# Prompt attention in head pairs inside the decode sequences, with page turns in three rotating half banks and the first pages loaded during the q projection

## The reference

```python
q = rms_norm((xn @ w_q).reshape(B, T, H, Dh), q_norm)
s = einsum('bqhd,bkhd->bhqk', q, k) * scale + f_q[..., None] - f_key
s = where(k_pos <= q_pos, s, -inf)
o = einsum('bhqk,bkhd->bqhd', softmax(s), v)          # then h += o @ w_o
# prompt: k, v are the 256 new tokens; f is the running sum of the log forget values
# decode: k, v = 1024 cached tokens (8 pages of 128, found through page_table) + 8 new ones
```

## Time and profile before

| | |
|---|---|
| median of 3 runs | 1751.15 us (1748.93 to 1753.79) |
| the profiled execution | 1752.86 us, span 1751.2 us |
| TensorE busy, of the span | 94% |
| VectorE, ScalarE, GpSimd busy | 57%, 37%, 5% |
| moved by DMA | 254.95 MB, 146 GB/s on average |
| granted TensorE clock, mean | 0.97 of full |

### The profile page before, as it was taken

The page is one execution under the profiler, slowest core; times in us unless marked ns, Lnnn a source line. Parts: engine busy times, 40 slices in busy tenths (PEclk is TensorE's granted clock), DMA queues, the critical chain, the costliest instruction groups (busy, mean ns, idle before and its releaser), DMA issues.

```text
span 1751.2 us, 37118 instructions
## 1 busy us (share of the span) xinstructions
PE 1648.4 (94%) x15372; PEld 1531.5 (87%) x15372; DVE 992.6 (57%) x1578; ACT 651.4 (37%) x935; POOL 90.3 (5%) x132
## 2 busy tenths in 40 slices
PE   6999999999999999999999999997778888999997
PEld 5999998988998999999889999984555566999997
DVE  5655437857774665544585555466744444655532
ACT  4343325643334543433433343331323332534320
POOL 0000000012212000000014300000000000000000
PEclk9999999999998999999999999996889998999999
DMA  6444462410002644444444444431079995444441
GB/s 188 146 156 155 133 180 73 145 61 16 16 16 59 190 145 144 148 152 146 131 156 152 150 154 146 154 102 48 13 290 350 352 371 185 145 145 156 149 143 62
DMA packets 206844, 254.95 MB, mean 146 GB/s; under 512 B 17914, under 2 KB 188074, under 8 KB 206586
## 3 DMA queue, kind: packets, MB, share of 16 engines
q1 hardware_dynamic: 202714, 246.38, 41.5%
q0 software_dynamic: 4016, 6.88, 1.4%
HBM read 246.89 MB, written 6.35 MB: 145 GB/s over the span
## 4 chain that ended last, share of the span: by engine, by line
PE 81%; DVE 10%; DMA 5%; ACT 2%; issue 2%; SPq 0%; POOL 0%; DVEq 0%; POOLq 0%
PE ps L691 20%; PE ps L692 20%; PE ps L690 20%; PE ps L945 7%; PE ps L940 4%; DMA ring<-in_cache_k 4%; PE ps L1253 2%; DVE ring_r L1658 2%; PE ps L1238 1%; ACT ring_r L1320 1%; DMA arena<-in_x_sample 1%; PE ps L1233 1%; DVE xn_r L1673 0%; PE ps L1126 0%; PE ps L805 0%
## 5 line engine op out<-in xcount | busy, mean ns | idle before, releaser
L690 PE MATMUL ps<-arena_r,ring_r 128*128 128x320 f32 x2032 | 632.5, 311 | 5.1 <-DVE xn_r L1673 3.1
L692 PE MATMUL ps<-arena_r,ring_r 128*128 128x320 f32 x2032 | 629.4, 310 | 0.0
L1658 DVE TENSOR_TENSOR ring_r<-ring,ring_r 128x2048 fp32r<-128x2048 f32 (+1 forms) x130 | 291.4, 2242 | 247.9 <-ACT ring_r L1320 144.9
L690 PEld LDWEIGHTS ps<-arena_r,ring_r 128*128 128x128 f32 x2032 | 383.1, 189 | 8.3 <-DVE ring_r L1658 3.5
L692 PEld LDWEIGHTS ps<-arena_r,ring_r 128*128 128x128 f32 x2032 | 383.1, 189 | 0.0
L691 PE MATMUL ps<-arena_r,ring_r 128*128 128x320 f32 x1136 | 351.0, 309 | 0.0
L691 PE MATMUL ps<-xn_r,ring_r 128*128 128x320 f32 x896 | 278.6, 311 | 0.0
L691 PEld LDWEIGHTS ps<-arena_r,ring_r 128*128 128x128 f32 x1136 | 213.3, 188 | 0.2
L1658 DVE TENSOR_TENSOR arena_r<-arena,arena_r (+3 forms) x155 | 141.9, 923 | 110.8 <-ACT arena_r L1320 49.5
L690 PE MATMUL ps<-arena_r 128*128 128x320 f32 x592 | 183.2, 309 | 0.0
L692 PE MATMUL ps<-arena_r 128*128 128x320 f32 x592 | 182.9, 309 | 0.0
(11 more groups left out here) (316 smaller groups left out, 2000.4 us busy)
## 6 DMA issues: line engine op xcount, KB each, us to landing
ring<-in_ffn_w_in SPq DMA_DIRECT2D x67, 1024.0 KB, 5.0
ring<-in_cache_k SPq DMA_DIRECT2D x64, 512.0 KB, 6.2
arena<-in_cache_v SPq DMA_DIRECT2D x64, 512.0 KB, 7.6
ring<-in_ffn_w_out SPq DMA_DIRECT2D x24, 1024.0 KB, 5.1
arena<-in_ffn_w_in SPq DMA_DIRECT2D x21, 1024.0 KB, 5.0
ring<-in_rw_w_rkv SPq DMA_DIRECT2D x11, 1024.0 KB, 5.1
ring<-in_ffn_w_out SPq DMA_DIRECT2D x12, 768.0 KB, 4.4
arena<-in_ffn_w_out SPq DMA_DIRECT2D x8, 1024.0 KB, 5.1
```

The source lines that it names most:

```text
L690: pe.matmul(out, part(s, 1)[:, k, cs], x_hi, start=first_, stop=False)
L692: return pe.matmul(out, part(s, 0)[:, k, cs], x_hi, start=False, stop=last)
L1658: return TT(out, x, high.bitcast(F32), ALU.subtract)
```

## The change

- `fox` leaves the list of tiles. The prompt attention of heads 2b and 2b+1 is done inside sequence b of the decode, in bank 6 (`FOX`), with semaphores of its own. The loops over sequences are written out on TensorE, ScalarE and VectorE.
- The scores read `q_f` and `kT` of the head's 64 partitions directly, without block-diagonal copies. The forget sums are kept as three fp32r parts in 48 rows for each half of the array (`nF`, `head_pick`) and enter by one fp32r matmul. A new tile `nf_rep` and eight small VectorE steps in `query_forgets` build them. `head_sel` and its DMA are gone.
- The values of a pair are written to the two partition halves of the bank and leave in one copy; `oT` is split block by block (`out_high`, `out_low`).
- Half page n (n = 2 for each page) goes to bank 3 + n % 3, instead of two pairs of banks.
- Seven value pages are loaded when `down2` is done, key pages 0 to 3 after the first slab of q, and pages 0 and 1 are turned before `q_rep`. The first two `fo` slabs are loaded after q and split within sequences 0 and 1.

```diff
@@ tiles and constants
+    add("nf_rep", 1)
-    add("fox", 3 * H)
+    m["fsel"] = (i[:, None] < H) & (i[:, None] == hd[None, :]) & (part[None, :] < 3)
+    m["fpart"] = part[:, None] == np.arange(3)[None, :]
+    m["fpick"] = (part[:, None] < 3) & (hd[:, None] == np.arange(H)[None, :])
+        PAGE_BANKS, FOX, OUT = 3, 6, 7
+        def page_bank(b, j, half):
+            return PAGE_BANKS + (2 * (b * PAGES + j) + half) % 3
@@ SyncE
+            sp.wait_ge(tile_done, first["down2"] + DT)
+            for j in range(PAGES - 1):
+                load_values_first(j)
+            sp.wait_ge(tile_done, first["q"] + 2)
+            for j in range(4):
+                load_k(0, j, page_of(0, j))
+            sp.wait_ge(S("page_space"), 1)
+            load_values_first(PAGES - 1)
+            for q in range(2):
+                s = first_slab["fo"] + q
+                load_slab(s, cols(dense["fo"], 0, DT, 256 * q, 256))
+                free_after(s, tile_done, first["fo"] + 2 * q + 2)
+            for j in range(4, PAGES):
+                load_k(0, j, page_of(0, j))
+            for j in range(4):
+                load_k(1, j, page_of(1, j))
+            with sp.Fori(1, BS - 1) as b:
                 load_sequence(b, False)
@@ TensorE
+            end(mmul(bank(t, TP), K("fsel")[0:H, :], FT_[:, 0:TP]))
+            def turn_page(b, j):
+                G = b * PAGES + j
+                pe.wait_ge(S(f"k_page{j % 4}"), b * 32 + 16 * (j // 4 + 1))
+                for half in range(2):
+                    if half == 0 and G >= 2:
+                        pe.wait_ge(S("kT_dve"), G - 1)
+                    if half == 1 and G >= 1:
+                        pe.wait_ge(S("kT_act"), G)
+                    for m in range(4):
+                        mm = pe.transpose(ps[:, page_bank(b, j, half), m * P:(m + 1) * P],
+                                          k_page(j % 4)[:, (4 * half + m) * P:(4 * half + m + 1) * P], ident)
+                mm.then_inc(S("k_page_free"), 1)
+            turn_page(0, 0)
+            turn_page(0, 1)
+            page_evicted(2, 2)
+            head_rep("q_rep", rs)
+            dve_done(first["q_rep"] + DT - 1)
+            turn_page(0, 2)
+            turn_page(0, 3)
+            def fox_scores(hd):
...
+                pe.matmul(ps[:, FOX, 0:3 * P], head_pick[pr, hd:hd + 1].to_broadcast([HD, P]), nF[pr, :],
+                          start=True, stop=False, skip_group_check=True)
+                pe.matmul(ps[:, FOX, 0:P], q_f[pr, m, 0:P], kT[pr, m, 0:P], start=False, stop=False,
                           skip_group_check=True)
+                pe.matmul(ps[:, FOX, P:3 * P], q_f[pr, m, P:2 * P], kT[pr, m, 0:2 * P], start=False, stop=True,
+                          skip_group_check=True).then_inc(S("fox_scores"), 1)
+            def fox_turn(hd):
+                pe.wait_ge(S("p_ready"), hd + 1)
+                if hd % 2:
+                    pe.wait_ge(S("fox_pT"), hd)
+                else:
+                    pe.wait_ge(S("fox_scored"), hd + 2)
...
+            def fox_values(m):
+                pe.wait_ge(S("fox_pT"), 2 * m + 2)
...
             def unit_scores(b, u):
-                pe.wait_ge(S("kT_act"), b * PAGES + (2 * u + 4))
-                pe.wait_ge(S("kT_dve"), b * PAGES + (2 * u + 4))
+                page_evicted(b * PAGES + 2 * u + 2, b * PAGES + 2 * u + 2)
@@ TensorE, one sequence
                 unit_scores(b, 0)
                 turn_page(b, 4)
                 turn_page(b, 5)
+                fox_scores(2 * b)
                 unit_scores(b, 1).then_inc(S("half_scored"), 1)
                 turn_page(b, 6)
+                fox_scores(2 * b + 1)
                 turn_page(b, 7)
                 unit_scores(b, 2)
                 unit_scores(b, 3)
...
+                fox_turn(2 * b)
                 if not last:
                     turn_page(b + 1, 0)
+                fox_turn(2 * b + 1)
+                if not last:
                     turn_page(b + 1, 1)
...
+                fox_values(b)
                 if not last:
                     turn_page(b + 1, 2)
@@ ScalarE, one sequence
+                page_copy(b, 4)
+                page_copy(b, 5)
+                fox_exp(2 * b)
+                page_copy(b, 6)
+                fox_exp(2 * b + 1)
+                page_copy(b, 7)
                 act.wait_ge(S("less_max"), b + 1)
...
+                out_high(b)
+                if not last:
                     page_copy(b + 1, 3)
+                if b < 2:
+                    hi(first_slab["fo"] + b)
@@ VectorE
-            copy_out("q", q_f, between=(lambda: later_pages(0), lambda: later_pages(1), query_forgets), norm_name="mix1")
+            copy_out("q", q_f, 2, between=(lambda: later_pages(0), lambda: later_pages(1), query_forgets), norm_name="mix1")
@@ VectorE, one sequence
+                page_copy(b, 4)
+                page_copy(b, 5)
+                fox_scored(2 * b)
+                page_copy(b, 6)
+                fox_scored(2 * b + 1)
+                page_copy(b, 7)
                 dve.wait_ge(S("half_scored"), b + 1)
                 dve.tensor_reduce(sst[:, 0:1], ps[:, 0, :], AX.X, ALU.max)
+                probabilities(2 * b)
...
+                probabilities(2 * b + 1)
+                fox_columns(2 * b)
                 if not last:
                     page_copy(b + 1, 0)
+                fox_columns(2 * b + 1)
+                if not last:
                     page_copy(b + 1, 1)
...
+                fox_out(b)
                 if not last:
                     page_copy(b + 1, 2)
                     queries(b + 1)
...
+                out_low(b)
...
+                if b < 2:
+                    lo(first_slab["fo"] + b)
```

More of the change, by code:

```diff
@@ L1187, in _ @@
             end(mmul(bank(t, TS), K("selcol")[0:H, :], FT_[:, TP:T]))
+            t = first["nf_rep"]
+            begin(t)
+            end(mmul(bank(t, TP), K("fsel")[0:H, :], FT_[:, 0:TP]))
             gemm("q", xn_hi, xn_lo, xn_ready("mix1"), "mix1")
             head_totals("q_norm", q_sq, S("q_sq"))
-            head_rep("q_rep", sg[:, 1, :])
-            pe.wait_ge(S("head_sel_in"), 16)
-            pe.wait_ge(S("nF_ready"), 1)
-            def scores(hd):
-                t = first["fox"] + fox_tile(hd, 0)
-                begin(t)
-                pe.wait_ge(S("qp_ready"), hd // 2 + 1)
-                qp = qp_bd[:, hd // 2 % 2, hd % 2, :]
-                pe.matmul(bank(t, 384), head_sel[:, hd, :], nF_dup, start=True, stop=False, skip_group_check=True)
-                pe.matmul(ps[:, t % 8, 0:P], qp[:, 0:P], kT[:, hd // 2, 0:P], start=False, stop=False,
-                          skip_group_check=True)
-                end(pe.matmul(ps[:, t % 8, P:3 * P], qp[:, P:2 * P], kT[:, hd // 2, 0:2 * P], start=False, stop=True,
-                              skip_group_check=True))
@@ L1223, in _, with page_evicted @@
-            for kind, hd in fox_order:
-                (scores, turn, values)[kind](hd)
+            def page_evicted(act_n, dve_n):
+                pe.wait_ge(S("kT_act"), act_n)
+                pe.wait_ge(S("kT_dve"), dve_n)
+            def turn_page(b, j):
[10 more added lines that the diff above has]
+                mm.then_inc(S("k_page_free"), 1)
@@ L1297, in sequence @@
                 pe.wait_ge(S("o_own"), b * 2 + 2)
-                pe.transpose(ps[:, 7, 256:384], o_two, ident).then_inc(S("o_turned"), 1)
-            dve_done(first["fox"] + 3 * H - 1)
-            for j in range(4):
-                turn_page(0, j)
-            with pe.Fori(0, BS - 1) as b:
-                sequence(b, False)
-            sequence(BS - 1, True)
-            pe.wait_ge(S("o_split"), 2)
+                pe.transpose(ps[:, OUT, 256:384], o_two, ident).then_inc(S("o_turned"), 1)
+            pe.wait_ge(S("o_split"), BS + 1)
             gemm("fo", oT_hi, oT_lo)
@@ L1556, in _, with head_roots @@
             ffn(1)
-            def head_roots(name, src_name, src, dst, sq_sem, norm_name):
+            def head_roots(name, src_name, src, dst, sq_sem, norm_name, ahead=4, out=None):
                 for q in range(4):
-                    hi(first_slab[src_name] + q + 2)
+                    if q < ahead:
+                        hi(first_slab[src_name] + q + 2)
                     if q == 0:
@@ L2295, in _, with fox_columns, fox_out @@
-            dve.wait_ge(dve_freed, freed["d"][first["fox"] + 3 * H])
-            dve.wait_ge(S("o_hi"), 1)
-            low(oT_lo[:, :, 0:TP], oT[:, :, 0:TP], oT_hi[:, :, 0:TP]).then_inc(S("o_split"), 1)
+            def fox_columns(hd):
+                dve.wait_ge(S("fox_turned"), hd + 1)
+                CP(pT[:, hd % 2, :], ps[:, FOX, 0:3 * P]).then_inc(S("fox_pT"), 1)
+            def fox_out(m):
+                dve.wait_ge(S("fox_values"), m + 1)
+                CP(oT[:, m, 0:TP], ps[:, FOX, 0:TP]).then_inc(S("fox_out"), 1)
@@ new lines, in out_low, with queries @@
+            def out_low(m):
+                dve.wait_ge(S("o_hi"), m + 1)
```

(26 more changed lines are left out.)

292 lines of the change are left out of this document (122 added, 170 removed).

## The result

The changed kernel took 1697.86 us, the median of 4 runs (1694.73 to 1700.72), against 1752.06 us for the kernel before in the same session. The ratio is 0.9692 with an interval of 0.9668 to 0.9716: 3.1% faster, 54 us. The forecast was 1707, range 1682 to 1727.

A forecast was written before the change was run, and what follows sets the result against it. The decode was taken as set by page transfers, TensorE close behind. `fo` begins at 1195.5 + 197.4 + 30.6 + 1 + 4.5 = 1429.0 instead of 1473.57, 44.6 us earlier: 1707 us, range 1682 to 1727.

The forecast's parts named there:

- the walk: TensorE's work and waits followed in order through one decode sequence with a pair of prompt heads; 28.2 us against 24.00.
- Period: Time of one decode sequence, from `unit_scores(b, 0)` to the next; 28.2 us predicted, seven of them 197.4.
- The stall of page 5: In each sequence, the upper half of page 5 waits for ScalarE's copy of page 4's lower half; 0.45 us.
- Step 6: Late in each sequence: head turn, page turns, transposes of p and `fox_values` (1.50 us), reaching 22.2 us.
- The wait for the turned head: In each sequence, TensorE idles 2.0 us while VectorE does `probabilities(2b+1)` and `fox_columns(2b)` before the head's turn.
- Clock: Allowance of 4.5 us because the first decode sequence would begin at TensorE's lower level, 1.2 GHz.
- Pages still pace it: Rival: in the decode, key pages end the waits and the period is 25.5 us; 1685 us, chance 0.13.
- A drain at each tile shape: Rival: switches to 64-row scores and 64-column values each drain TensorE, decode 8 us longer; 1715 us, chance 0.10.
- Low clock in the first sequences: Rival: TensorE at the lower clock through the first sequences, some 20 us more; 1727 us, chance 0.08.
- Slower: Rival: lower clock all through the decode because new 2 us gaps recur; 1867 us, chance 0.03.
- nothing: Rival: a decode period near 33.8 us eats the 44.6 us gain; chance 0.01.
- steps 3 to 5: Sequence waits: page 4's copy 0.45 us, page 7's copy behind the exponentials 1.0, VectorE before the head's turn 2.0.

The follow-up runs named there:

- copy7_first: The changed kernel with ScalarE copying page 7 ahead of the exponentials of head 2b+1; 1692.12 us, ratio 0.9654.
- values_128: The changed kernel with the pair's values computed on all 128 weight columns, one head after the other, two copies out; 1705.74 us, ratio 0.9728.
- no_prompt: The changed kernel with the prompt attention left out of the sequences, its block of oT filled with zeros; 1680.55 us, ratio 0.9585.
- reordered2: The changed kernel with page copies, head turns, probabilities, pair values and the turn of `o_two` reordered across TensorE, ScalarE and VectorE; 1677.75 us, ratio 0.9572.
- late_pages: The changed kernel with key pages 0 to 3, all eight first value pages and `fo` issued only at `page_space`; 1711.88 us, ratio 0.9764.
- fp32_forget: The changed kernel with the forget part of the prompt scores in fp32 instead of fp32r; 1706.62 us, ratio 0.9752.

## Why the prediction was right

The mechanism was right: the waits of the walk stand where it put them, and pages no longer end them. The result was 9 us high. More than half of that, 5.5 us, are two allowances beside the walk that were not needed (4.5 for the clock, 1 for the splits); the rest are sizes taken a little large. One reading of the earlier trace rows was wrong, that a new tile shape has no price, and the walk hit some numbers by luck; both are told below.

- **First unit.** Predicted 1195.5, measured 1195.37. This close a hit is luck, since two errors cancel: the q product ended at 1181.4 instead of 1179.8, and the turns of pages 0 and 1 and `q_rep` ran faster than priced, at full clock (granted 1.00 up to 1191.90, `q_rep` 1.36 us). Behind the wait of 3.26 us the clock was down as priced: pages 2 and 3 took 3.47 us at a granted clock of 0.52.
- **Period.** 28.2 against 27.56 (the later ones 27.64, and the seventh 29.25). To the end of the new tokens' scores 13.8 was walked and 13.74 is measured, and that too is luck in part: the two stalls are shorter by 0.5 and the scores' own matmuls by 0.2, while the old work around them takes 0.6 more than the 10.17 of the earlier trace rows, where a wait or a new tile shape cuts a group. In it the fp32r pass is 0.28, not 0.18: the row of a 320-column projection matmul did not carry over to this one. The stall of page 5 is 0.25 for 0.45, the one for page 7 is 0.71 for 1.0. `copy7_first` shows the latter's cause.
- **Step 6** is the part of the walk most mis-sized: `fox_values` 0.81 for 1.50. I took twice the price of a head from the earlier trace rows, whose matmuls follow one another on the whole array. `values_128` shows that working in two column halves in turn makes the difference. The wait for the turned head is 1.65 for 2.0, by the same order on VectorE as walked.
- **Clock.** 4.5 us were set aside for the first sequence, and it cost 0: granted clock 1.00 from 1195.37 to 1222.94. The prediction held both views, 4.5 us in the sum and "2.4 GHz from the first sequence on" among its signs; the second came true. The seventh sequence (29.25, granted 0.94) and the last (29.05, granted 0.90) pay instead, some 1.6 us in the seventh.
- **Last sequence.** 30.6 predicted, 29.05 measured, with the idle at the place named (2.52) and the lower clock behind it. The two splits of `fo` cost nothing that shows, where I had 1.
- **Sum.** 197.4 + 30.6 + 1 + 4.5 = 233.5 was set against 224.1 measured: 2.4 from the seven periods, 1.5 from the last, 1 and 4.5 from the rest. These make 9.4 and, with 0.1 at the first unit, 9.5 at `fo`; of that, 0.5 is gone again by the end.

**The rivals.** *Pages still pace it*: no, since no page is waited for; but in `no_prompt` they do at once, and `reordered2` is at the edge. *A drain at each tile shape*: true in kind, though not in size. The three products of a head take 1.02 us from the first start to the next group's (1199.28 to 1200.30, and 1202.97 to 1203.99), less than the 1.1 of the sum. But their neighbours got longer. Eight transposes hold TensorE for 0.93 us ahead of a group of 128x128 (1203.99 to 1204.92) and for 1.03 ahead of the 64-row scores (1201.94 to 1202.97). The first group of a unit takes 0.64 behind the scores (1200.30 to 1200.94) and 0.54 behind a page turn (1204.92 to 1205.46). And the 64-column values start 0.20 behind the last transpose of p, where the 128-column ones of `values_128` start after 0.11. That is about 0.1 us at each of four places, 0.4 a sequence and some 3 us in all, where the prediction gave the rival 8. This agrees with the Trainium skill, page "TensorEngine Tiling (Array Packing)", section "Key Properties", which the prediction named, as far as that a change of tiling mode has a cost. *Low clock in the first sequences*: not in this kernel; in `late_pages` it stands behind a wait of 8.99 us (granted 0.72 from 1213 to 1230). *Slower* and *nothing*: the three new waits of steps 3 to 5 came out below their price, and `fp32_forget` shows that work added there comes through once, 0.94 a sequence, and does not multiply.

**Where the gain came from.** The attention of the prompt, some 70 us on the path, costs 17 where it lies beside the pages (`no_prompt`). Around it three smaller pieces each carry a part, measured by undoing that one: early pages 14 us by the medians, `fo` out of q 14 (some 10 in the trace), the forget sums in one pass 8.8 (7.5 by the periods). They cannot be added up, for each was undone alone.

**Open.** How much of the 54 us the cheaper attention (no block-diagonal queries, one fp32r pass, 64-column values) would give in its old place, ahead of the decode: no run has it there. And what makes the clock fall in one sequence and not in the next. In the kernel before it held through a gap of 2.43 us in the earlier trace rows, and fell behind one of 2.69 in its first sequence (granted 0.88 from 1276.19 to 1304); after, it fell once behind a gap of 1.65 that it outlasts in the six other sequences, and in `no_prompt` it fell behind gaps of 2.4 us. No run separates the causes.

## What to carry to other kernels

Where one stage waits for transfers and another for engines, laying one beside the other is worth more than starting the transfers early (54 against 2 to 4 us here); price it by walking the program of the fullest engine in order, with each wait that the other engines' orders bring. After that the gaps that remain come from the order of the programs, on the helper engines and on the full one, and swapping calls there is cheap: three rounds of it gave 20 us more. Price a change of tile shape at some 0.1 us, and look at the group ahead of it for that time. When they are gone the transfers are the bound again, so know their time per round beforehand.

## What the hardware showed unexpectedly

- Matmuls that use 64 weight columns in alternating halves of the array are cheaper than the same work on 128: 12 of 128 moving columns in 0.81 us against 1.34.
- A new tile shape costs TensorE about 0.1 us, and it shows on the neighbour: eight transposes take 0.93 us from start to next start ahead of a 128x128 group and 1.03 ahead of the 64-row scores.
- Fewer bytes need not mean less DMA time: half the partitions of the value pages gave 228 instead of 303 GB/s at a share of 0.84 against 0.79 (1222.94 to 1390), while half of each row in all partitions took `reordered2` from 336 to 258 GB/s and the share from 0.89 to 0.72 (1221 to 1371).
- The lower clock outlives the wait that goes before it: behind 1.95 us in `reordered2` the next three groups took longer (1.42 for 1.09, 1.56 for 0.88, 1.66 for 1.09), so that the sequence lost 3.5 us (27.65 against the 24.17 of one without waits) and not 1.95.
